# Down products in two matmuls a tile, their residual additions on VectorE, and a new hand-laid chunk order in a two-layer trunk

## What is computed

```python
def swiglu(h, w_gate, w_up, w_down):
    return (jax.nn.silu(h @ w_gate) * (h @ w_up)) @ w_down

def reference(x, ...):
    for l in range(DEPTH):
        ...
        x = x + swiglu(rms_norm(x, ffn_norm[l]), w_gate[l], w_up[l], w_down[l])
    return rms_norm(x, final_norm)
```

## Time and profile before

| | us |
|---|---|
| median of 3 runs | 1746.88 |
| lowest, highest | 1745.84, 1747.18 |
| the profiled execution | 1745.04 |
| its span | 1743.2 |
| feed-forward of layer 0, first chunk to first product of the last down stage | 39.6 to 717.8 |
| the same of layer 1 | 1013.2 to 1687.8 |

### The profile page before, as it was taken

One profiled execution on the slowest core, in us unless ns is written; L12 is line 12 of the kernel. 1 busy time (PEld: TensorE's weight loads), 2 busy tenths in 40 slices (PEclk: granted clock), 3 DMA queues, 4 the chain that ended last, 5 costly groups with the idle time before them and its releaser, 6 DMA issues.

```text
span 1743.2 us, 32496 instructions
## 1 busy us (share of the span) xinstructions
PE 1721.5 (99%) x12816; PEld 1632.9 (94%) x12816; DVE 1403.0 (80%) x1765; ACT 1151.0 (66%) x1753; POOL 222.3 (13%) x244
## 2 busy tenths in 40 slices
PE   9999999999999999999999999999999999999998
PEld 6888999999999999889999888899999999999997
DVE  5898777788877887798997779787778888878766
ACT  6656667677776676566775456576767766767753
POOL 2100000001000000364112420000000000000000
PEclk9999999999999999999999999999999999999999
DMA  6677878788888896755445457787887788879772
GB/s 227 213 235 210 255 229 256 241 246 246 246 252 245 243 302 160 248 188 161 148 139 170 156 183 225 225 257 230 251 265 222 237 253 252 243 229 267 224 250 94
DMA packets 111020, 388.81 MB, mean 223 GB/s; under 512 B 12448, under 2 KB 13856, under 8 KB 110752
## 3 DMA queue, kind: packets, MB, share of 16 engines
q1 hardware_dynamic: 94464, 327.03, 51.8%
q0 software_dynamic: 16128, 58.73, 19.4%
q10 hardware_dynamic: 288, 1.11, 0.2%
HBM read 326.01 MB, written 2.10 MB: 188 GB/s over the span
## 4 chain that ended last, share of the span: by engine, by line
PE 85%; DVE 11%; ACT 1%; DMA 1%; issue 1%; SPq 0%; DVEq 0%; ACTq 0%
PE ps L705 17%; PE ps L706 9%; PE ps L907 9%; PE ps L909 9%; PE ps L910 9%; PE ps L713 7%; PE ps L715 7%; PE ps L717 7%; DVE w_lo L1719 5%; DVE raw L1809 2%; PE ps L790 2%; PE ps L724 1%; PE ps L725 1%; PE ps L726 1%; ACT w_hi L1264 1%
## 5 line engine op out<-in xcount | busy, mean ns | idle before, releaser
L1719 DVE TENSOR_TENSOR w_lo<-raw,w_hi 128x1024 fp32r<-128x1024 f32 (+2 forms) x793 | 944.4, 1199 | 269.9 <-ACT w_hi L1264 267.3
L1264 ACT ACTIVATE w_hi<-raw 128x1024 fp32r<-128x1024 f32 (+2 forms) x794 | 816.4, 1034 | 211.5 <-PE ps L706 137.1
L705 PE MATMUL ps<-xg,w_hi 128*128 128x512 f32 x1088 | 383.6, 393 | 4.6 <-DVE w_lo L1719 4.6
L713 PE MATMUL ps<-act,w_hi 128*128 128x256 f32 x1152 | 321.9, 279 | 0.2 <-DVE w_lo L1719 0.2
L715 PE MATMUL ps<-act,w_hi 128*128 128x256 f32 x1152 | 322.0, 279 | 0.0
L717 PE MATMUL ps<-act,w_lo 128*128 128x256 f32 x1152 | 321.4, 279 | 0.0
L706 PE MATMUL ps<-xg,w_lo 128*128 128x256 f32 x1088 | 306.5, 282 | 0.0
L907 PE MATMUL ps<-w_hi,mix_hi_lo 128*128 128x256 f32 x896 | 254.4, 284 | 7.5 <-DVE w_lo L1719 7.3
L910 PE MATMUL ps<-w_hi,mix_hi_lo 128*128 128x256 f32 x896 | 251.7, 281 | 0.0
L909 PE MATMUL ps<-w_lo,mix_hi_lo 128*128 128x256 f32 x896 | 251.7, 281 | 0.0
L705 PEld LDWEIGHTS ps<-xg,w_hi 128*128 128x128 f32 x1088 | 204.3, 188 | 47.7 <-DVE w_lo L1719 7.1
(11 more groups left out here) (252 smaller groups left out, 2637.5 us busy)
## 6 DMA issues: line engine op xcount, KB each, us to landing
raw<-w_stream SPq DMA_DIRECT2D x224, 512.0 KB, 5.0
raw<-w_group SPq DMA_DIRECT2D x224, 512.0 KB, 6.4
raw<-raw POOLq DMA_DIRECT2D x112, 512.0 KB, 5.5
raw<-w_stream SPq DMA_DIRECT2D x64, 384.0 KB, 4.9
raw<-w_o SPq DMA_DIRECT2D x32, 512.0 KB, 3.3
raw<-w_down SPq DMA_DIRECT2D x28, 512.0 KB, 6.3
raw<-w_q_a SPq DMA_DIRECT2D x8, 512.0 KB, 3.2
raw<-w_kv_a SPq DMA_DIRECT2D x8, 512.0 KB, 3.3
```

The costliest lines, as they stand in the source:

```text
L705: pe.matmul(ps[:, bank, :], w_hi[:, s, j * P:(j + 1) * P], moving, start=start, stop=False)
L713: pe.matmul(dst, w_hi[:, s, j * P:(j + 1) * P], moving[:, 0:SEQ], start=False, stop=False, skip_group_check=True)
L1264: nc.scalar.activation(dst, src, ACT.Copy).then_inc(hi_ready, 1)
L1719: nc.vector.tensor_tensor(lo, src, hi.bitcast(F32), ALU.subtract).then_inc(lo_ready, 1)
```

## The change

1. The order of a layer's chunks is a string, `ORDER`, one letter a chunk; `up_order` only numbers the letters. Plain and down chunks stand mostly singly between group chunks.
2. Stage 2 has 3 groups and no plain tile (2 and 2 before): 15 groups a layer, 30 in all. A layer has 210 group, 56 plain and 80 down chunks, 346 in all.
3. A down chunk uses `product3`: per tile one matmul of 512 and one of 256 columns, from an empty bank. VectorE adds both halves of the bank into x (`down_out_of`). ScalarE's `seed` and `seeded_out` are gone. A down chunk's first matmul waits for the addition of the second down chunk before it.
4. The list ends with 4 plain chunks, and two down chunks ahead of them.

```diff
-STAGE_GROUPS = (0, 3, 2, 3, 3, 3)
+STAGE_GROUPS = (0, 3, 3, 3, 3, 3)
...
+ORDER = (
+    "PPPPPPPPPPPPPPPPPPPPPPSPSSSSSSPSSSSSPPSSSPSSPSSSPSSPPPSSSSDSSDSDDSDSDSSD"
...
+    "SSDSSDDSDDSSSSSSSDSSDDDSSSDSDSSDSDSDSSSSDDSPSDSSDPSPDDPPPP"
+)
 def up_order():
+    turn = {
+        "S": iter([("S", g, r, c) for g in range(LAYER_GROUPS) for r in PRODUCTS for c in range(2)]),
+        "P": iter([("P", p, c) for p in range(LAYER_PLAIN) for c in range(4)]),
+        "D": iter([("D", s, d) for s in range(STAGES - 1) for d in range(DT)]),
+    }
+    return [next(turn[kind]) for kind in ORDER]
...
             def down_chunk(layer, k):
...
-                pe.wait_ge(seeded, before + 1)
+                if before >= 2:
+                    pe.wait_ge(down_out, before - 1)
                 for j in range(STAGE_TILES[s]):
-                    mm = product_onto(n, j, down_bank(layer, before), act[:, act_slot(s, j), :], j == STAGE_TILES[s] - 1)
+                    mm = product3(n, j, down_bank(layer, before), act[:, act_slot(s, j), :], j == 0, j == STAGE_TILES[s] - 1)
...
-            def seed(layer, k):
-
-                d, before = UP_ORDER[k][2], downs_before(layer, k)
...
-                nc.scalar.activation(ps[:, down_bank(layer, before), 0:SEQ], x[:, d, :], ACT.Copy).then_inc(seeded, 1)
-
-            def seeded_out(layer, k):
-
-                sc.wait_ge(chunks_used, done_at(layer, k))
-                nc.scalar.activation(x[:, UP_ORDER[k][2], :], ps[:, down_bank(layer, downs_before(layer, k)), 0:SEQ],
-                                     ACT.Copy).then_inc(down_out, 1)
...
+            def down_out_of(layer, k, d):
+
+                bank, xd = down_bank(layer, downs_before(layer, k)), x[:, d, :]
+                ve.wait_ge(chunks_used, done_at(layer, k))
+                step(nc.vector.tensor_tensor(xd, ps[:, bank, 0:SEQ], xd, ALU.add))
+                nc.vector.tensor_tensor(xd, ps[:, bank, SEQ:], xd, ALU.add).then_inc(down_out, 1)
...
                         if g is not None:
                             group_act(g)
+                        d = down_ended(at)
+                        if d is not None:
+                            down_out_of(layer, at, d)
                     split_up(CHUNK[UPS[layer]] + k + SPLIT_SLOTS)
```

48 lines of the change are left out of this document (3 added, 45 removed).

## The result

The changed kernel takes **1765.36 us** (median of 4 runs, 1764.16 to 1766.24) where the kernel before takes 1746.36 (4 runs; the forecast started from 1746.88, the median of three of them): a ratio of 1.0112, 95% interval 1.0100 to 1.0124. It is 1.1% slower. The forecast was 1736, with a range that ended at 1743. The profiled run has a span of 1763.5 us.

What follows compares the result with a forecast made beforehand. TensorE's instruction stream plus few gaps was taken as the bound (99% busy). Terms -3.3 - 4.0 - 11.9 + 8.2 = -11.0 us took the median 1746.88 to 1735.9, rounded 1736; range 1726 to 1743.

Steps and rivals of the forecast that it cites:

- Part 1: Down products as 512 + 256 on TensorE: 1152 tiles, each from 0.3494 to 0.3466 us, -3.3 us.
- Part 2: Stage 2: one more group in each layer replaces two plain tiles, 20.24 against 22.24 us; -4.0 us for two layers.
- Part 3: Down chunks: ScalarE's copies go, VectorE adds 126 us, covered where it would have waited for ScalarE's half; no loss counted.
- Rival 4: VectorE becomes the bound: additions delay splits; a fifth of 126 us shows on top of rival 3's 1748, 1773; chance 0.06.
- the small gaps outside of the two places: Later VectorE debts in the new order, priced at 1.5 us a layer.
- Part 4: New order of chunks: VectorE's debts shrink, so TensorE's gaps mostly go; -11.9 us, between -5 and -15.
- two gaps at the first P5 and P6: At the first group, VectorE's debt from the mixing steps meets P5 and P6 without plain chunks between: 1.6 us a layer.
- the four gaps of the earlier trace: TensorE gaps at VectorE's debts, chunks 42 to 46, 143, 208, 275: 4.5, 0.6, 1.2, 1.7 us; expected to go.
- Rival 2: Waits for data: W11's addition and reload, 12.5 us in 13.3, and the first down product; 1738 to 1742; chance 0.13.
- the rival's other window: First down product comes 5.6 us after the last early plain tile, whose chain needs about 5.2.
- Part 5: Layer's end: waits for down additions, 1.2 us, and for the last group's activation, 2.9 us, a layer; +8.2 us.

Runs made afterwards that it cites:

- experiment 1: Changed kernel with the order and 14 groups a layer of the kernel before, keeping the new down products and VectorE's additions; 1751.48 us.
- experiment 3: Changed kernel with chunks 87 to 104 and 153 to 176 laid evenly, group and down chunks mixed, same letters; 1745.15 us.
- experiment 12: Changed kernel with its layer end repaired and the same 346 chunks in a new order, laid by DMA and VectorE budgets; 1723.09 us.
- experiment 9: Changed kernel in the old order with 14 groups a layer, VectorE's two additions of a down chunk cut to 16 of 256 columns; 1746.14 us.
- experiments 6 to 8 and 10: Changed kernel without W21 += W11 (1750.79 us); with half the bytes in quarter loads (1742.61); in DMA additions (1748.09); with VectorE's down additions on 16 columns (1754.72).
- experiment 4: Changed kernel with the layer's last two down chunks two chunks earlier and the group's activation ahead of the plain tile's sums; 1755.93 us.

## Why the prediction was wrong, step by step

**Part 1, the form: the pace right, the gain a little too large.** A tile of the changed kernel takes 0.347 us, as forecast (six tiles from 501.76 to 503.84 in a down chunk of layer 0). But the forecast set a step from a down chunk to another kind (2.795 us) against one between two plain chunks (2.773), which has no change of kind in it. The changed kernel's step from a down chunk to a group chunk is 2.786. In the same order (experiment 1) the 160 chunks gain 2.5 us, not 3.3.

**Part 2, the group: right.** Without their waits the two stretches take 1328.8 us in experiment 1 (14 groups a layer) and 1324.6 in experiment 3 (15): 4.1 us less, 4.0 forecast. The order of experiment 12 contains it too, and its sum closes to 1.5 us: 1745.0 - 2.5 - 4.0 - 18.1 (all gaps gone) + 1.5 (two waits left at the end) + 3.2 (small gaps left) = 1725.1 us, and its profiled execution took 1723.6.

**Part 3, VectorE's additions "covered": about 8 us uncovered in the old order, little in the new one.** The step was "this is covered where VectorE would have waited for ScalarE's half". It holds for most of the 160 chunks: 126 us of work cost 8. Where VectorE was late already (chunks 145, 211, 277, 294) the additions came on top, 0.5 to 1.1 us each. Rival 4 named this mechanism with a share of a fifth of 126 us; it is a sixteenth. In the new order the debts had been reckoned with the additions in them, and this isn't the main part of the miss: the small gaps outside of the two places are 3.4 us, 3.0 forecast. VectorE's busy time rose by 68.7 and 69.8 us a stretch (78 forecast), ScalarE's fell by 38.1 and 38.3 (54 forecast). Experiment 1 parts the terms. The additions bring VectorE 59 us a stretch, not 67, and the group about 10 (11 forecast). The copies take 43 us off ScalarE's busy time, not the 60.5 of their durations: instructions that follow each other are drawn overlapping, and busy time counts the overlap once. The group brings ScalarE 4.5 us (6 forecast).

**Part 4, the order: the step that failed.** The sum had nothing in it for waits for data. The places forecast did come: two gaps at the first P5 and P6, 3.1 us (3.2), and the four gaps of the earlier trace rows are gone. The second of them in the changed kernel:

```profile
114.29 0.39 PE L882 MATMUL ps<-w_hi,mix_hi_lo 128*128 128x256 f32 x1 [0.59 <-DVE w_lo L1675]
```

What was not in the sum is 26.8 us in the two dense places. Rival 2 named the mechanism and one window, P2 to the next P1 between groups 6 and 7, and priced it at 1 to 3 us a layer with a chance of 0.13. The two places cost 13.4 a layer, that window 3.8 and 2.9 us of it; the rival's other window, the first down product, cost nothing. Its terms were the *medians* of the earlier trace rows, 5.5 and 6.4 us, read over the whole kernel; beside the other loads of the run the second addition took 8.5 us and the reload 8.5 and 7.5. In the trace of before, the longest addition takes 9.4 us and the longest quarter load 9.4 as well, so a margin of 0.8 us in 13.3 could not be called enough (the working's own paces give 13.4). And the windows of the first place, half of the loss, are in no rival: P2 to P4 of one group, with the addition between them and eleven group chunks in a row, and five down chunks on three slots, whose fourth load must wait for the split of the first and then land in a full DMA system.

**Part 5, the end of a layer: right, a little small.** Forecast 1.2 and 2.9 us a layer, lost 1.6 and 3.2:

```profile
711.65 0.47 PE L690 MATMUL ps<-xg,w_hi 128*128 128x512 f32 x1 [1.47 <-DVE x L1823]
```

```profile
726.51 0.47 PE L690 MATMUL ps<-act,w_hi 128*128 128x512 f32 x1 [3.08 <-DVE act L1815]
```

```profile
724.83 0.69 DVE L1786 TENSOR_TENSOR sums<-sums,rstd 128x512 f32<-128x512 f32 x1
725.44 0.68 DVE L1815 TENSOR_TENSOR act<-ps,act 128x512 fp32r<-128x512 f32 x1
```

The group's activation does stand behind the two sums, as the order said. The 0.3 that is missing is on TensorE: it starts 0.39 us after L1815's end (725.44 + 0.68), where I had 0.1. The 0.4 of the other wait is an instruction that the order of the streams shows and I passed over: the half of a plain tile's activation, L1795, stands ahead of the additions and holds them up by 0.33 us.

```profile
710.29 0.42 DVE L1795 TENSOR_TENSOR act<-product,act 128x256 fp32r<-128x256 f32 x1
710.62 0.42 DVE L1822 TENSOR_TENSOR x<-ps,x 128x256 f32<-128x256 f32 x1
```

And layer 0 pays once more behind the wait, outside of the table: the granted clock is 0.50 from 728 to 730 and five tiles take 0.64, about 1.5 us.

```profile
728.00:730.00 2.00, 2.00 (x7) 1.70 (x7) 1.11 (x1) 0.00 (x0) 0.00 (x0) 0.50 0.00 0
```

**The range.** It took in rival 2 at 1742. With the longest rows of before (9.4 us for an addition and 9.4 for the reload, against 13.3) the same working gives 5 to 6 us for that window in each layer, and the upper end would have passed before's time.

**What stays open.** How the 3 us of experiment 9 arise that don't go with the additions' length, how much of the first place is the three slots and how much the full DMA system (no run has more slots), and how the gains of experiments 6 to 8 and 10 divide: they add up to more than the two places lose, since each shortens the same chain (addition, load, split, addition in VectorE's queue, bank).

## What to carry to other kernels

When a change makes one kind of work denser, make the account of that stretch for *every* engine that serves it, DMA's 16 engines too, in busy time per unit of work (here 23.9 us of DMA in a group's 20.2 us of TensorE). A mean share of 0.80 hides it, and a median latency belongs to the mean load. A margin in a window that is smaller than the spread of its terms is no margin; price it with the longest such row. Ask of every ring of buffers how many chunks in a row want it. And when a change that should pay doesn't, look at the sum without its waits: here it was 2.5 + 4.0 + 18.1 = 25 us better than before, and another order of the same chunks brought 22 of them.

## What the runs showed of the hardware

- An addition by DMA within SBUF costs the DMA engines 2.1 times what a load of the same 512 KB does (3.07 against 1.45 us of all 16), and windows in which additions run are full at half the rate: 198 GB/s at a share of 1.03, against 412 to 414 GB/s behind them.
- Its time from issue to landing is 4.6 us for the first of a pair and 8.1 to 8.5 us for the second, beside which five quarter loads were issued (median of all 5.5, longest 10.3). A stream load of 512 KB takes 6.5 us in such a stretch and 2.9 us just behind it.
- A wait of TensorE can cost a second time. In the changed kernel the granted clock fell to 0.50 (the 1.2 GHz level) at waits of 1.78, 3.08 and 3.98 us (249, 726 and 1240 us), for 3 to 7 us, with 1.6, 1.5 and 2.5 us lost beside the wait. It did not fall at a wait of 2.24 us (374), nor at one of 2.09 (260), nor at one of 3.08 at the end of layer 1 (1709). In the trace of experiment 4 the same waits at 261 (2.08 us) and 377 (2.21 us) did bring it down. So neither the length of a wait nor its place tells it; a forecast needs an upper bound of 2.5 us on top of each such wait. Windows behind the wait at 261, in the changed kernel and in experiment 4:

```profile
261.00:263.00 2.00, 2.00 (x13) 1.76 (x12) 1.97 (x4) 0.00 (x0) 0.00 (x0) 1.00 0.69 193
```

```profile
262.00:264.00 2.00, 2.00 (x7) 1.67 (x7) 1.97 (x4) 0.00 (x0) 0.00 (x0) 0.50 0.69 184
```

The wait at 1709, behind which the clock stayed at 1.00:

```profile
1708.96 0.47 PE L690 MATMUL ps<-act,w_hi 128*128 128x512 f32 x1 [3.08 <-DVE act L1815]
```
